# Feed-forward input products of two transformer blocks: high and low activations in one 512-column product, the second half of the bank copied by ScalarE

## The chip, the cores and the metric

The kernel runs as one program on one core of a Trainium2 chip. The metric is the device time of one execution in microseconds (us), the median of several runs. The engines are named as in the profile: PE is TensorE's matmul, PEld its weight load, DVE is VectorE, ACT is ScalarE, POOL is GpSimd, SP is SyncE, which issues most DMAs.

## The reference, cut to what matters

Two blocks of a transformer on one sequence of 256 tokens, D_MODEL = 1024, all in fp32. The first block has four feed-forward parts of this form (D_FF = 2816), before and after its mixers:

```python
def _swiglu(h, w_in, w_out):
    a, b = jnp.split(h @ w_in, 2, axis=-1)
    return (jax.nn.silu(a) * b) @ w_out
```

h is the RMS-normed x (256 x 1024) and w_in is 1024 x 5632. The change touches only the product h @ w_in of these four parts and what directly follows it. The second block's own MLPs (squared ReLU) are not touched.

## The kernel before, in words

**Products in three terms.** Activations and weights are kept as pairs of fp32r tiles, a high part (the value rounded by a copy) and a low part (what the rounding left). A product is the sum of three: high weight x high activation, high weight x low activation, low weight x high activation. For the feed-forward input they are issued by `product` (lines 1878 to 1880) through `two_chunks`, on 256 tokens = 256 columns each. The activations' parts lie in two tiles, `h_hi` and `h_lo`. In the last stage of the program (`mlp_latent`, lines 2448 and 2449) another form is used: activations in one tile `g_both` of two halves, one product of 512 columns for both halves and one of 256 for the low weight, both into one bank.

**Weights in panels.** All weights come as panels of 1 MB (128 x 2048) or 704 KB (128 x 1408, feed-forward outputs), in two buffers. For each panel SP loads `raw`, ACT copies it to `w_hi` in two halves (`hi`, line 617) and DVE subtracts to `w_lo` in two halves (`lo`, line 1057, each after its half of `w_hi`). ACT may write into a buffer only after PE is done with the panel that lay there (`gemm_done`). PE waits for both halves of `w_lo` (`lo_ready`).

**A feed-forward input** has 22 units, one panel each: 128 gate columns a and 128 up columns b, that is 2 x 8 chunks of K x 3 = 48 matmuls. The first unit is peeled (`first_chunks`, lines 1923 to 1925; it goes along with the norm). The others are in a loop of two units per iteration (j = 0 and 1). After each j = 0 unit PE does 64 tiny matmuls of another weight (`ada`, line 1987). a and b of a unit lie in the two halves of one PSUM bank, 0 or 1 by turns. Unit n + 2 may begin when unit n's bank is released (`bank_free`).

**What follows a unit** (`swiglu_evac` on DVE, `swiglu` on ACT) starts when the whole unit is done:

1. DVE: a times the norm's reciprocal (line 1099).
2. ACT: tanh of a/2 (line 704). DVE meanwhile does the low part of the unit before (`low`, line 1086).
3. DVE: (tanh + 1) times a (line 1105), then times b from PSUM (line 1110), which releases the bank.
4. ACT: the copy to the high part of g (line 706).

**The order is written by hand.** The program order of ACT for the unit p is: convert panel p + 1 (two of line 617), tanh of unit p, copy of unit p, then convert panel p + 2. That of DVE is: two of line 1057 for panel p + 1, then the steps of unit p. So the conversion of panel p + 2 on ACT stands behind the copy of unit p on ACT, and on DVE unit p's steps stand behind the low part of panel p + 1.

After 22 units the outputs follow (`out_of`, lines 1966 to 1968), 16 panels of 704 KB with 33 matmuls each.

## Time and profile before

| | |
|---|---|
| median of 3 runs | 2270.43 us (2269.54 to 2276.41) |
| the profiled execution's own time | 2277.8 us |
| its span, first to last instruction | 2276.1 us |
| PE busy, share of the span | 2146.5 us, 94% |
| PEld | 1872.6 us, 82% |
| DVE | 1387.3 us, 61% |
| ACT | 846.5 us, 37% |
| POOL | 38.2 us, 2% |
| granted TensorE clock, mean | 0.965 |
| chain that ended last | PE 82%, DVE 10%, ACT 4% |

The profiled execution took 7.4 us more than the median. Matmuls are pipelined: a row of PE shows the matmul's whole stay, so what counts is the distance of two starts. The same holds, less strongly, on DVE and ACT: an instruction that needs nothing of the one before it starts some 0.08 us before that one's recorded end.

### The profile page before, as it was taken

How to read it: one execution, taken by the hardware profiler on the slowest of the kernel's cores; microseconds unless marked ns; L12 is line 12 of the kernel's file. 1: busy time of each engine (PE TensorE's matmuls, PEld its weight loads, DVE VectorE, ACT ScalarE, POOL GpSimd, SP SyncE). 2: the span in 40 equal slices, each digit the busy share in tenths (PEclk: the TensorE clock that was granted, in tenths of full speed). 3: DMA queues.
4: the chain of work that ended last, by engine and by line, in shares of the span. 5: the costliest groups of instructions: out<-in, count | busy, mean ns of one | idle time of the engine just before them, and what ended most of it. 6: DMA issues, size and time to landing. Idle time of an engine off the chain costs nothing.

```text
span 2276.1 us, 42979 instructions
## 1 busy us (share of the span) xinstructions
PE 2146.5 (94%) x17118; PEld 1872.6 (82%) x17118; DVE 1387.3 (61%) x2295; ACT 846.5 (37%) x1336; POOL 38.2 (2%) x60
## 2 busy tenths in 40 slices
PE   7999899999999998999979999899999989999998
PEld 7999778999999998899966676787887865458987
DVE  6666667666666667766654556674265355557854
ACT  4444534444444443444422434411111223234332
POOL 0000000000000000000010000000000000000000
PEclk9999989999999999999999999999999989799999
DMA  7665325665666632566531110222222222003544
GB/s 267 237 229 200 138 74 185 238 241 183 235 247 209 224 135 94 193 235 234 205 136 38 38 38 20 80 99 86 110 92 93 93 74 92 1 19 114 182 169 144
DMA packets 50227, 325.71 MB, mean 143 GB/s; under 512 B 5328, under 2 KB 8656, under 8 KB 16976
## 3 DMA queue, kind: packets, MB, share of 16 engines
q1 hardware_dynamic: 42480, 266.62, 33.1%
q0 software_dynamic: 7648, 57.71, 6.7%
q8 instruction: 70, 1.15, 0.2%
q14 instruction: 29, 0.24, 0.0%
HBM read 323.26 MB, written 1.05 MB: 142 GB/s over the span
## 4 chain that ended last, share of the span: by engine, by line
PE 82%; DVE 10%; ACT 4%; issue 2%; DMA 0%; DVEq 0%; ACTq 0%; SPq 0%
PE psum L1878 17%; PE psum L1879 16%; PE psum L1880 16%; PE psum L1966 4%; PE psum L1968 3%; PE psum L1967 3%; PE psum L2448 3%; DVE w_lo L1057 3%; PE psum L1987 2%; PE psum L2292 2%; ACT w_hi L617 1%; PE psum L2449 1%; ACT scratch L863 1%; PE psum L2277 1%; PE psum L2312 1%
## 5 line engine op out<-in xcount | busy, mean ns | idle before, releaser
L1057 DVE TENSOR_TENSOR w_lo<-raw,w_hi 128x1024 fp32r<-128x1024 f32 (+1 forms) x542 | 600.0, 1147 | 236.5 <-ACT w_hi L617 221.7
L617 ACT ACTIVATE w_hi<-raw 128x1024 fp32r<-128x1024 f32 (+1 forms) x542 | 514.5, 991 | 574.9 <-PE psum L1880 351.6
L1878 PE MATMUL psum<-h_hi,w_hi 128*128 128x256 f32 (+1 forms) x2136 | 644.4, 302 | 18.2 <-DVE x_res L1217 6.3
L1879 PE MATMUL psum<-h_lo,w_hi 128*128 128x256 f32 (+1 forms) x2136 | 636.4, 298 | 0.0
L1880 PE MATMUL psum<-h_hi,w_lo 128*128 128x256 f32 (+1 forms) x2136 | 635.9, 298 | 0.0
L1878 PEld LDWEIGHTS psum<-h_hi,w_hi 128*128 128x128 f32 x2136 | 413.3, 193 | 39.7 <-issue 17.1
L1880 PEld LDWEIGHTS psum<-h_hi,w_lo 128*128 128x128 f32 x2136 | 413.8, 194 | 10.0
L1879 PEld LDWEIGHTS psum<-h_lo,w_hi 128*128 128x128 f32 x2136 | 413.9, 194 | 9.8
L1966 PE MATMUL psum<-g_both,w_hi 128*128 128x256 f32 x704 | 202.4, 287 | 8.2 <-DVE w_lo L1057 8.2
L1967 PE MATMUL psum<-g_both,w_hi 128*128 128x256 f32 x704 | 199.1, 283 | 0.0
L1968 PE MATMUL psum<-g_both,w_lo 128*128 128x256 f32 x704 | 199.1, 283 | 0.0
L1966 PEld LDWEIGHTS psum<-g_both,w_hi 128*128 128x128 f32 x704 | 134.9, 192 | 13.4 <-DVE w_lo L1057 12.8
L1967 PEld LDWEIGHTS psum<-g_both,w_hi 128*128 128x128 f32 x704 | 134.9, 192 | 0.0
L1968 PEld LDWEIGHTS psum<-g_both,w_lo 128*128 128x128 f32 x704 | 134.9, 192 | 0.0
L704 ACT ACTIVATE scratch<-scratch 128x256 f32<-128x256 f32 x88 | 36.8, 418 | 213.9 <-DVE scratch L1099 213.9
L854 ACT ACTIVATE scratch<-psum 128x512 f32<-128x512 f32 x80 | 43.4, 594 | 171.9 <-PE psum L2292 171.9
L1577 DVE SCALAR_TENSOR_TENSOR x_res<-psum,mods,x_res 128x256 f32<-128x256 f32 (+1 forms) x64 | 28.0, 478 | 129.8 <-PE psum L1880 118.5
L1878 PE MATMUL psum<-g_both,w_hi 128*128 128x512 f32 x256 | 100.3, 392 | 6.1 <-DVE g_both L1718 6.1
L1880 PE MATMUL psum<-g_both,w_lo 128*128 128x512 f32 x256 | 100.3, 392 | 0.0
L1879 PE MATMUL psum<-g_both,w_hi 128*128 128x512 f32 x256 | 100.3, 392 | 0.0
L2448 PE MATMUL psum<-g_both,w_hi 128*128 128x512 f32 x256 | 92.1, 404 | 3.2 <-DVE g_both L1718 3.2
L2449 PE MATMUL psum<-g_both,w_lo 128*128 128x256 f32 x256 | 72.6, 283 | 0.0
(345 smaller groups left out, 3193.4 us busy)
## 6 DMA issues: line engine op xcount, KB each, us to landing
raw<-in_weights SPq DMA_DIRECT2D x207, 1024.0 KB, 4.8
raw_ada<-in_ada POOLq DMA_DIRECT2D x48, 1024.0 KB, 6.7
raw<-in_weights SPq DMA_DIRECT2D x64, 704.0 KB, 4.1
arena<-in_rpb POOLq DMA_DIRECT2D x1, 2048.0 KB, 11.3
arena<-in_fox_c POOLq DMA_DIRECT2D x1, 1696.0 KB, 9.1
const_region<-in_latent_c POOLq DMA_DIRECT2D x1, 1394.0 KB, 7.2
const_region<-in_even_c POOLq DMA_DIRECT2D x1, 1360.0 KB, 8.0
x_res<-in_x_lat SPq DMA_DIRECT2D x4, 256.0 KB, 7.2
```

What stands on the lines that cost most here:

```text
L617: nc.scalar.activation(wh[s][:, a], raw[s][:, a], ACT.Copy).then_inc(hi_ready, 1)
L1057: V.tensor_tensor(wl[s][:, a], raw[s][:, a], wh[s][:, a].bitcast(F32), ALU.subtract).then_inc(lo_ready, 1)
L1878: mm(out, sh, mh, start=n == 0, stop=False)
L1879: mm(out, sh, ml, start=False, stop=False)
L1880: ins = mm(out, sl, mh, start=False, stop=n == len(pairs) - 1)
L1966: mm(out, wh[s][:, a:a + P], gh[:, g0:g0 + T], start=first, stop=False)
L1967: mm(out, wh[s][:, a:a + P], gl[:, g0:g0 + T], start=False, stop=False)
L1968: ins = mm(out, wl[s][:, a:a + P], gh[:, g0:g0 + T], start=False, stop=last)
L1987: ins = mm(psum[r:r + 32, ADA_BANK, 0:64], cond_s[:, c, :], own, start=c == 0, stop=c == DC - 1, tile_position=(0, r))
L2292: ins = nc.tensor.transpose(psum[:, 4 + m, b * P:(b + 1) * P], st_p[:, 2 * (k % 2) + m, b * P:(b + 1) * P], ident)
L2448: mm(out, wh[s][:, a:a + P], g_both[:, :, g0:g0 + T], start=first, stop=False)
L2449: ins = mm(out[:, 0:T], wl[s][:, a:a + P], gh[:, g0:g0 + T], start=False, stop=last)
```

## The change

- The high and low activations lie in one tile `h_both` (two halves), and `h_hi` and `h_lo` are views of it. Other stages use the views as before.
- A unit of the feed-forward inputs now uses two banks, 0 or 1 for the gate and 4 or 5 for the up part. Per chunk of K there is one matmul of 512 columns (high weight with both halves of the activations, into the whole bank) and one of 256 (low weight with the high activations, into the bank's first half). So 32 matmuls instead of 48; the columns are as many as before. All gate matmuls come first, then all up matmuls. The first unit's gate uses bank 3.
- Each result is now the sum of a bank's two halves. ACT copies the second half to SBUF (two new copies per unit), and DVE adds it to the first (two new additions per unit): the gate's sum into `n_add`, the up part's into `e_tmp`. The line that multiplied with b in PSUM now reads `e_tmp`.
- The gate signals on its own (`gate_done`), half a unit before `gemm_done`. The bank is released after the up sum.

```diff
-        hh = sb("h_hi", [P, DC, TJ], F32R)
-        hl = sb("h_lo", [P, DC, TJ], F32R)
+        h_both = sb("h_both", [P, 2, DC, TJ], F32R)
+        hh, hl = h_both[:, 0, :, :], h_both[:, 1, :, :]
...
+        ffn_gl, ffn_ul = n_sq[:, 0, :], n_sq[:, 1, :]
...
             def swiglu(i, j):
 
                 n = pos.n("unit") + 2 * i + j
+                first = isinstance(i, int) and i == 0 and j == 0
+                b = (pos.u + j) % 2
+                act.wait_ge(gate_done, n + 1)
+                nc.scalar.activation(ffn_gl, psum[:, FFN_FIRST if first else b, T:TJ], ACT.Copy).then_inc(gate_low, 1)
                 act.wait_ge(scaled_a, n + 1)
                 nc.scalar.activation(ffn_t[:, j, :], ffn_a[:, j, :], ACT.Tanh, scale=0.5).then_inc(tanh_done, 1)
-                act.wait_ge(bank_free, pos.u + 2 * i + j + 3)
+                act.wait_ge(gemm_done, pos.e + 2 * i + j + 1)
+                nc.scalar.activation(ffn_ul, psum[:, UP + b, T:TJ], ACT.Copy).then_inc(up_low, 1)
+                act.wait_ge(ffn_made, n + 1)
                 nc.scalar.activation(flat(gh, (2 * i + j) * T, T), ffn_g[:, j, :], ACT.Copy).then_inc(g_hi_done, 1)
...
-                    dve.wait_ge(gemm_done, pos.e + 2 * i + j + 1)
-                    V.tensor_tensor(ffn_a[:, j, :], ps_a, n_inv, ALU.mult).then_inc(scaled_a, 1)
+                    dve.wait_ge(gate_low, n + 1)
+                    V.tensor_tensor(n_add, ps_a, ffn_gl, ALU.add).then_inc(gate_sum, 1)
+                    dve.wait_ge(gate_sum, n + 1)
+                    V.tensor_tensor(ffn_a[:, j, :], n_add, n_inv, ALU.mult).then_inc(scaled_a, 1)
...
                     V.scalar_tensor_tensor(ffn_u[:], ffn_t[:, j, :], 1.0, ffn_a[:, j, :], ALU.add,
                                            ALU.mult).then_inc(ffn_seq, 1)
+                    dve.wait_ge(up_low, n + 1)
+                    V.tensor_tensor(e_tmp[:], ps_b, ffn_ul, ALU.add).then_inc(bank_free, 1)
                     dve.wait_ge(ffn_seq, n + 1)
+                    freed(u)
                     if not peeled:
                         dve.wait_ge(g_ready, n - 1)
-                    V.tensor_tensor(ffn_g[:, j, :], ffn_u[:], ps_b, ALU.mult).then_inc(bank_free, 1)
+                    V.tensor_tensor(ffn_g[:, j, :], ffn_u[:], e_tmp[:], ALU.mult).then_inc(ffn_made, 1)
...
+            def wide_chunks(b, s):
+
+                for m, (o, done) in enumerate(((b, gate_done), (UP + b, gemm_done))):
+                    for k in range(DC):
+                        w_hi, w_lo = wtile(s, k, m, 2 * P)
+                        both, low = (psum[:, o, :], w_hi, h_both[:, :, k, 0:T]), (psum[:, o, 0:T], w_lo, hh[:, k, 0:T])
+                        if k < DC - 1:
+                            mm(*both, start=k == 0, stop=False)
+                            mm(*low, start=False, stop=False)
+                        else:
+                            mm(*low, start=False, stop=False)
+                            ins = mm(*both, start=False, stop=True)
+                    ins.then_inc(done, 1)
```

Where the instructions move: DVE in the loop over units, first iteration's j = 0 unit, from the second half of the low weights on. Names: `w_lo` the low weights, `scratch` holds a, tanh, u and g, `norm_blk` holds the reciprocal and the new copies and the gate's sum, `rope_tmp` is `e_tmp`. Before:

```order
L1057 TENSOR_TENSOR w_lo<-raw,w_hi 128x1024 [waits hi_ready]
L1099 TENSOR_TENSOR scratch<-psum,norm_blk 128x256 [waits gemm_done]
...
L1086 TENSOR_TENSOR g_both<-scratch,g_both 128x256
L1078 REGISTER_ALU
L1105 SCALAR_TENSOR_TENSOR scratch<-scratch 128x256 [waits tanh_done,bank_free]
L1110 TENSOR_TENSOR scratch<-scratch,psum 128x256 [waits g_ready,ffn_seq]
```

And with the change:

```order
L1067 TENSOR_TENSOR w_lo<-raw,w_hi 128x1024 [waits hi_ready]
L1109 TENSOR_TENSOR norm_blk<-psum,norm_blk 128x256 [waits gate_low]
L1111 TENSOR_TENSOR scratch<-norm_blk 128x256 [waits gate_sum]
...
L1096 TENSOR_TENSOR g_both<-scratch,g_both 128x256
L1088 REGISTER_ALU
L1117 SCALAR_TENSOR_TENSOR scratch<-scratch 128x256 [waits tanh_done,bank_free]
L1120 TENSOR_TENSOR rope_tmp<-psum,norm_blk 128x256 [waits up_low]
L1088 REGISTER_ALU [waits ffn_seq]
L1125 TENSOR_TENSOR scratch<-scratch,rope_tmp 128x256 [waits g_ready,bank_free]
```

The gate's sum (L1109) still stands behind the low weights of the next panel (L1067), and the scaling (L1111) now waits for a result of its own engine.

ACT at the same unit, before:

```order
L704 ACTIVATE scratch<-scratch 128x256 [waits scaled_a]
L705 REGISTER_ALU
L706 ISA [waits bank_free]
L706 ACTIVATE g_both<-scratch 128x256
L614 ISA
L617 ACTIVATE w_hi<-raw 128x1024 [waits gemm_done,raw_loaded0]
```

And with the change:

```order
L710 ACTIVATE norm_blk<-psum 128x256 [waits gate_done]
L712 ACTIVATE scratch<-scratch 128x256 [waits scaled_a]
L714 ACTIVATE norm_blk<-psum 128x256 [waits gemm_done]
L716 ISA [waits ffn_made]
L716 ACTIVATE g_both<-scratch 128x256
L618 ISA
L621 ACTIVATE w_hi<-raw 128x1024 [waits gemm_done,raw_loaded0]
```

The two copies (L710, L714) stand around the tanh, and the next panel's conversion (L621) still stands last, behind the copy to g's high part (L716).

## Rows read from the trace of the kernel before

**Rows 1.** The page: busy times, chain that ended last.
```profile
PE 2146.5 (94%) x17118; PEld 1872.6 (82%) x17118; DVE 1387.3 (61%) x2295; ACT 846.5 (37%) x1336; POOL 38.2 (2%) x60
PE 82%; DVE 10%; ACT 4%; issue 2%; DMA 0%; DVEq 0%; ACTq 0%; SPq 0%
```

**Rows 2.** Stretches: us, busy time of each engine, clock, DMA share, GB/s. One iteration.
```profile
36.74:49.48 12.74, 12.74 (x167) 12.52 (x161) 8.06 (x14) 5.57 (x8) 0.53 (x1) 1.00 0.62 239
```

**Rows 3.** Timeline of PE, 256-column matmuls of an input unit.
```profile
42.12 0.28 PE L1880 MATMUL psum<-h_hi,w_lo 128*128 128x256 f32 x1
42.24 0.28 PE L1878 MATMUL psum<-h_hi,w_hi 128*128 128x256 f32 x1
42.36 0.28 PE L1879 MATMUL psum<-h_lo,w_hi 128*128 128x256 f32 x1
```

**Rows 4.** Timeline of PE, last stage: first and last of 32 wide matmuls.
```profile
2194.84 0.40 PE L2448 MATMUL psum<-g_both,w_hi 128*128 128x512 f32 x1
2195.07 0.28 PE L2449 MATMUL psum<-g_both,w_lo 128*128 128x256 f32 x1
...
2205.78 0.40 PE L2448 MATMUL psum<-g_both,w_hi 128*128 128x512 f32 x1
```

**Rows 5.** Timeline of ACT, one iteration (start, duration, line, idle before and releaser).
```profile
43.26 0.42 ACT L704 ACTIVATE scratch<-scratch 128x256 f32<-128x256 f32 x1 [3.13 <-DVE scratch L1099]
44.79 0.42 ACT L706 ACTIVATE g_both<-scratch 128x256 f32 x1 [1.11 <-DVE scratch L1110]
45.21 2.01 ACT L617 ACTIVATE w_hi<-raw 128x1024 fp32r<-128x1024 f32 x2
49.03 0.42 ACT L704 ACTIVATE scratch<-scratch 128x256 f32<-128x256 f32 x1 [1.81 <-DVE scratch L1099]
50.56 0.42 ACT L706 ACTIVATE g_both<-scratch 128x256 f32 x1 [1.11 <-DVE scratch L1110]
50.89 1.99 ACT L617 ACTIVATE w_hi<-raw 128x1024 fp32r<-128x1024 f32 x2
```

**Rows 6.** Timeline of DVE, the same iteration.
```profile
42.80 0.42 DVE L1099 TENSOR_TENSOR scratch<-psum,norm_blk 128x256 f32<-128x256 f32 x1 [1.23 <-PE psum L1880]
...
46.30 2.36 DVE L1057 TENSOR_TENSOR w_lo<-raw,w_hi 128x1024 fp32r<-128x1024 f32 x2 [1.57 <-ACT w_hi L617]
48.58 0.42 DVE L1099 TENSOR_TENSOR scratch<-psum,norm_blk 128x256 f32<-128x256 f32 x1
48.92 0.41 DVE L1086 TENSOR_TENSOR g_both<-scratch,g_both 128x256 f32 x1
49.55 0.43 DVE L1105 SCALAR_TENSOR_TENSOR scratch<-scratch 128x256 f32<-128x256 f32 x1 [0.22 <-ACT scratch L704]
50.02 0.42 DVE L1110 TENSOR_TENSOR scratch<-scratch,psum 128x256 f32<-128x256 f32 x1
```

**Rows 7.** One line of ACT: its reads of 128x256 from PSUM (min/median/max ns).
```profile
L737 ACT ACTIVATE arena<-psum,small x9: 467/484/517, 256.2 to 287.1; 128x256 f32<-128x256 f32 x8, 16x256 f32<-16x256 f32 x1
```

**Rows 8.** Waits: who waited for whom: us in total, times, longest.
```profile
DVE scratch L1099 <- PE psum L1880: 51.3, 44, 1.2
```

**Rows 9.** Timeline of ACT, first and last conversions beside the first input's loop.
```profile
26.28 1.99 ACT L617 ACTIVATE w_hi<-raw 128x1024 fp32r<-128x1024 f32 x2
...
159.77 1.46 ACT L617 ACTIVATE w_hi<-raw 128x704 fp32r<-128x704 f32 x2
```

**Rows 10.** Timeline of PE: the first unit and the first output panel that waited.
```profile
29.77 0.39 PE L1878 MATMUL psum<-h_hi,w_hi 128*128 128x256 f32 x1 [1.16 <-DVE w_lo L1057]
...
162.33 0.39 PE L1966 MATMUL psum<-g_both,w_hi 128*128 128x256 f32 x1 [0.94 <-DVE w_lo L1057]
```

More of the change, by code:

```diff
@@ L60 @@
 FIRST = 4
+FFN_FIRST, UP = 3, 4
 def weight_plan():
@@ L240, in build @@
         ada_done = sem("ada_done")
+        gate_done, gate_low, gate_sum = sem("gate_done"), sem("gate_low"), sem("gate_sum")
+        up_low, ffn_made = sem("up_low"), sem("ffn_made")
         ada_turned = sem("ada_turned")
@@ L1093, in evac @@
                     bank = (pos.u + j) % 2
-                    ps_a, ps_b = psum[:, bank, 0:T], psum[:, bank, T:2 * T]
+                    ps_a, ps_b = psum[:, bank, 0:T], psum[:, UP + bank, 0:T]
                     if peeled and j == 0:
                         inverse_norm()
-                        ps_a, ps_b = psum[:, FIRST, 0:T], psum[:, FIRST + 1, 0:T]
-                    dve.wait_ge(gemm_done, pos.e + 2 * i + j + 1)
-                    V.tensor_tensor(ffn_a[:, j, :], ps_a, n_inv, ALU.mult).then_inc(scaled_a, 1)
+                        ps_a = psum[:, FFN_FIRST, 0:T]
+                    dve.wait_ge(gate_low, n + 1)
+                    V.tensor_tensor(n_add, ps_a, ffn_gl, ALU.add).then_inc(gate_sum, 1)
+                    dve.wait_ge(gate_sum, n + 1)
+                    V.tensor_tensor(ffn_a[:, j, :], n_add, n_inv, ALU.mult).then_inc(scaled_a, 1)
                     if not (peeled and j == 0):
@@ L1926, in first_chunks, with first_wide @@
                 return ins
+            def wide_chunks(b, s):
[10 more added lines that the diff above has]
+                    ins.then_inc(done, 1)
+            def first_wide(s):
+                for k in range(DC):
+                    if k == DC - 1:
+                        first_sum()
+                    pe.wait_ge(h_ready, pos.n("h", 1))
+                    for m, (o, done) in enumerate(((FFN_FIRST, gate_done), (UP + pos.u % 2, gemm_done))):
+                        w_hi, w_lo = wtile(s, k, m, 2 * P)
+                        both, low = (psum[:, o, :], w_hi, h_both[:, :, k, 0:T]), (psum[:, o, 0:T], w_lo, hh[:, k, 0:T])
+                        if k < DC - 1:
+                            mm(*both, start=k == 0, stop=False)
+                            mm(*low, start=False, stop=False)
+                        else:
+                            mm(*low, start=False, stop=False)
+                            ins = mm(*both, start=False, stop=True)
+                        if k == DC - 1:
+                            ins.then_inc(done, 1)
             def first_sum():
@@ L1945, in into @@
                     bank(pos.u + 2 * i + j)
-                    chunks = first_chunks if isinstance(i, int) and i == 0 and j == 0 else two_chunks
-                    chunks(psum[:, (pos.u + j) % 2, :], s).then_inc(gemm_done, 1)
+                    if isinstance(i, int) and i == 0 and j == 0:
+                        first_wide(s)
+                    else:
+                        wide_chunks((pos.u + j) % 2, s)
                     if j == 0:
```

## The prediction

> **What bounds the kernel now.** I read the page first: PE is busy 94% of the span and is 82% of the chain that ended last [rows 1]. Then one stretch, an iteration (two units) of a feed-forward input's loop: it takes 12.74 us, PE is busy in all of it at full clock, DVE 8.06 us and ACT 5.57 us [rows 2]. So PE sets the pace there. The matmuls of 256 columns start 0.12 us apart [rows 3]; 96 of them are 11.52 us, and the remaining 1.22 us are the 64 tiny ones of `ada` with the gaps around them. The average unit takes 6.37 us. The four inputs have 4 x 22 = 88 units.
>
> Then the timelines of ACT and DVE, because this engine pair feeds PE, and here one must look at order, not at busy shares. There is a circle through both. From the start of a panel's conversion on ACT (45.21) to the point where DVE is free after the low part (48.58) are 3.37 us [rows 5, 6]. From DVE's first step of a unit to ACT's next conversion are 2.41 us (42.80 to 45.21) and 2.31 us (48.58 to 50.89), mean 2.36 us; one of them has the loop's turn in it. Together 5.73 us per unit if nothing else is waited for. PE's 6.37 us are longer, so DVE waits for PE: 51.3 us in total, 44 times, at most 1.2 us [rows 8]. That is a margin of only 6.37 - 5.73 = 0.64 us per unit. **This small margin decides the case.**
>
> **The change on PE.** It removes three matmuls of 256 columns per chunk of K and puts one of 512 and one of 256 in their place. The same pair exists in the last stage, on a tile of two halves: 31 pairs take 2205.78 - 2194.84 = 10.94 us, 0.353 us each [rows 4], against 3 x 0.12 = 0.36 us [rows 3]. That is 0.007 us less, by 16 pairs and 88 units: 1408 x 0.007 = 9.8 us less work for PE. An iteration would need 32 x 0.353 + 1.22 = 12.52 us, 6.26 us per unit. The columns are as many as before, which is why so little is won by a third fewer matmuls.
>
> The Trainium skill (TensorE: Matmul & The Clock Gate, Back-to-back issue gap) gives a warm matmul of N columns N / 2.4 ns plus 2.5 ns. By it the pair saves one fixed part of 2.5 ns, an estimate of 3.5 us for all 1408. The trace differs: 0.12 us for 256 columns is some 11 ns more than the page gives, and the pair saves about 7 ns.
>
> **The change on DVE and ACT.** Each unit gets two additions on DVE and two copies on ACT. An addition of this shape lasts 0.42 us (as line 1099, which also reads PSUM and SBUF [rows 6]), a copy 0.42 us (as line 706 [rows 5]) up to 0.48 us (as the reads from PSUM in [rows 7]). What matters is what of it lies in the circle:
>
> - Gate copy on ACT: it stands directly behind the conversion, which ends at +2.0 us, while DVE works on the low part until +3.37 us [rows 5, 6]. Hidden, price 0. The early signal of the gate is worth nothing here: the data are there, but DVE's sum stands in its queue behind the low weights of the next panel, and those behind ACT's conversion.
> - Gate sum on DVE: the scaling now waits for it, a result of the same engine. The nearest pair is line 1105 to line 1110, 0.46 us (49.55 to 50.02, 0.47 as printed) [rows 6]. **+0.46 us.**
> - Up copy on ACT: it may start some 0.33 us after the tanh started (as 50.56 to 50.89 [rows 5]) and ends at 0.33 + 0.42 + 0.04 = 0.79 us, signal included. DVE is free for the up sum 0.52 us (tanh to line 1105, 49.03 to 49.55) + 0.34 us (48.58 to 48.92, two independent steps) = 0.86 us after the tanh's start [rows 5, 6]. Hidden; with 0.52 us, the maximum of [rows 7], it costs 0.03 us.
> - Up sum on DVE: it starts 0.34 us behind (tanh + 1) a, and the last product stands 0.46 us behind the up sum, as it stood 0.46 us behind (tanh + 1) a before. **+0.34 us.**
> - The waits: `gate_low`, `up_low`, `ffn_made` replace others. Where an instruction has a second wait, it starts 0.10 us after what it waited for (49.03 + 0.42 to 49.55), with one wait 0.04 us (42.80 + 0.42 to 43.26) [rows 5, 6]. For two new ones that is 0 to 0.12 us; I take 0, since each has one late wait.
>
> The circle becomes 5.73 - 0.01 + 0.46 + 0.34 = 6.52 us (3.36 instead of 3.37 for the conversion, because 48.58 is also the moment when PE was done). It is longer than what PE needs now (6.26) and longer than the unit before (6.37). **So the bound moves from PE to the circle of ACT and DVE**, and PE waits for `w_lo`, 0.5 us per iteration. Behind this wait nothing else of PE is due; the bank's release comes a unit early enough either way.
>
> **The sum.** For the first input the conversion behind unit 0 starts at 26.28 and that of the second output panel at 159.77, 133.49 us later [rows 9]. With the change unit 0's own steps are 0.80 us longer, then come 20 rounds of 6.52 us, and a last one that is 0.93 us shorter, because its panel is of 704 columns (conversion to PE 162.33 - 159.77 = 2.56 us against 29.77 - 26.28 = 3.49 us [rows 9, 10]): 0.80 + 130.4 + 5.59 = 136.8 us, 3.3 us more. PE already waited for exactly this conversion before (0.94 us at 162.33 [rows 10]), so the delay passes to it whole; from then on the outputs are PE's as before. Three more inputs of the same code: 4 x 3.3 = **13.2 us more**. The first unit's reordering costs nothing: it goes along with the norm, and the tanh's table, now loaded behind the gate copy, has the reciprocal to hide under. PE's 9.8 us turn into waiting and are worth nothing. Against the profiled execution's 2277.8 us that is 2291.0; against the median, 2270.43 + 13.2 = 2283.6 us.
>
> Bounds: if both sums pass on 0.04 us earlier (no signal time, 0.42 instead of 0.46), 84 rounds give 6.7 us back: +6.5 us. If both new waits cost 0.06 us more and the up copy 0.03 us, 84 x 0.15 = 12.6 us come on top: +26 us. The forecast's own range is 2277 to 2296.
>
> **The rivals.**
>
> - *PE stays the bound.* The circle is under 6.26 us, 0.26 us shorter than I sum. Then the whole 9.8 us are gained: 2260.6 us. For it: ACT has 5.57 of 12.74 us of work, with the copies 7.3, and DVE 8.06 + 1.7 = 9.8 us, all under 12.52; by busy time alone nothing binds. Against: every step of the circle is read from rows of the same loop, and none is 0.26 us too long. By the page's 2.5 ns this rival's time would be 2266.9 us. Chance 0.11.
> - *The circle binds, but softly.* It is 6.26 to 6.44 us, because some step starts before its predecessor's end more than the rows show: between 9.8 us gained and 6.5 us lost, middle about 2269 us. Chance 0.13.
> - *The new waits are dear.* Register steps and double waits add over 0.15 us per unit, or ACT and PE slow each other in PSUM: over 2296 us, at 0.25 us extra 84 x 0.25 = 21 us on top, 2305 us. For it: the last product now has three waits. Chance 0.08.
> - *The wide product is no faster than two of 256.* Rows 4 speak against it; PE would need 6.37 us per unit, which is still under 6.52, so the forecast stands even then.
>
> **How the numbers follow.** Forecast 0.68, softly 0.13, PE-bound 0.11, dear 0.08. About 0.3% (6.8 us) is what a measurement can tell from no change: 2263.6 to 2277.2. Faster: most of the PE-bound case and the edge of the soft one, 0.10. Same: the rest of the soft case, a weak gain and the forecast's lowest edge, 0.19. Slower: 0.71. The range goes up to the forecast's bound, 2296, and down to 2267, which leaves out the dear case and most of the PE-bound one, somewhat under 0.2.
>
> **What would show it.** In the profile after: an iteration of the inputs takes about 13.04 us instead of 12.74; PE has new idle time before the first matmul of every second unit, released by the low weights on DVE, about 0.5 us each; pairs of matmuls 0.353 us apart; the waits of DVE for the gate's signal gone or nearly; the gate's scaling 0.46 us after its sum, and ACT's conversion 6.5 us after the one before. It is wrong if PE shows no such waits (first rival), or if the step from up sum to the last product is far over 0.46 us (third).

## The result, and the profile after

| | before | with the change |
|---|---|---|
| median, same chip | 2273.42 us (6 runs, 2268.99 to 2279.59) | 2296.06 us (6 runs, 2288.73 to 2298.20) |
| the profiled execution's own time, its span | 2277.8, 2276.1 us | 2296.21, 2294.6 us |
| ratio | | 1.0099, 95% interval [1.0079, 1.0119] |

The kernel is **slower by 22.5 us** (18 to 27 by the interval). The two profiled executions differ by 18.4 us. The forecast was 13.2 us more, with 2296 as the upper end. Sign and mechanism hold, the size does not.

First the page: busy times, the chain that ended last, and the group of the wide matmuls.

```profile
PE 2143.7 (93%) x15710; PEld 1798.0 (78%) x15710; DVE 1450.9 (63%) x2471; ACT 893.9 (39%) x1512; POOL 38.1 (2%) x60
...
PE 60%; DVE 21%; ACT 10%; issue 7%; ACTq 1%; DVEq 0%; DMA 0%; SPq 0%
...
L1950 PE MATMUL psum<-h_both,w_hi 128*128 128x512 f32 x1176 | 431.6, 405 | 20.1 <-DVE w_lo L1067 20.1
```

PE's busy share fell by one point only. The chain tells more: PE was 82% of it [rows 1] and is 60% now, DVE and ACT together went from 14% to 31%. In the inputs more of this chain now runs through the two small engines. The wide matmuls wait 20.1 us for the low weights.

Two iterations of two units in the first input, an early and a later one, and one in the second input (columns as in [rows 2]). They are cut at ACT's conversions:

```profile
37.09:50.10 13.01, 13.01 (x133) 11.20 (x132) 9.51 (x19) 6.75 (x12) 0.53 (x1) 1.00 0.68 243
98.58:111.59 13.01, 12.78 (x131) 10.74 (x130) 9.52 (x19) 6.64 (x12) 0.53 (x1) 1.00 0.67 244
450.52:463.65 13.13, 12.69 (x130) 10.71 (x130) 9.52 (x18) 6.66 (x13) 0.53 (x1) 1.00 0.62 242
```

It was 12.74 us; the forecast was 13.04. The first input has 13.01, the later ones have 13.13. No engine is full in the last two stretches: in the second input PE works 12.69 and DVE 9.52 of 13.13 us. A circle binds, not a busy engine. In the first stretch PE shows no idle time, because it has fallen behind: it began with a wait of 2.25 us (below), and the `ada` matmuls that close its iterations are there 12.50 us apart (38.19 and 50.69), while ACT's rounds already take 13.01. Only from 83.02 on does it wait in every iteration of this input.

The circle itself, in the later stretch of the first input. ACT's timeline:

```profile
99.08 2.01 ACT L621 ACTIVATE w_hi<-raw 128x1024 fp32r<-128x1024 f32 x2
100.99 0.36 ACT L710 ACTIVATE norm_blk<-psum 128x256 f32<-128x256 f32 x1
103.36 0.42 ACT L712 ACTIVATE scratch<-scratch 128x256 f32<-128x256 f32 x1 [2.01 <-DVE scratch L1111]
103.69 0.36 ACT L714 ACTIVATE norm_blk<-psum 128x256 f32<-128x256 f32 x1
105.23 0.42 ACT L716 ACTIVATE g_both<-scratch 128x256 f32 x1 [1.18 <-DVE scratch L1125]
105.55 1.99 ACT L621 ACTIVATE w_hi<-raw 128x1024 fp32r<-128x1024 f32 x2
```

And DVE's, over the same round:

```profile
100.17 2.36 DVE L1067 TENSOR_TENSOR w_lo<-raw,w_hi 128x1024 fp32r<-128x1024 f32 x2 [1.55 <-ACT w_hi L621]
102.45 0.42 DVE L1109 TENSOR_TENSOR norm_blk<-psum,norm_blk 128x256 f32<-128x256 f32 x1
102.90 0.42 DVE L1111 TENSOR_TENSOR scratch<-norm_blk 128x256 f32<-128x256 f32 x1
103.25 0.42 DVE L1096 TENSOR_TENSOR g_both<-scratch,g_both 128x256 f32 x1
103.88 0.42 DVE L1117 SCALAR_TENSOR_TENSOR scratch<-scratch 128x256 f32<-128x256 f32 x1 [0.22 <-ACT scratch L712]
104.23 0.42 DVE L1120 TENSOR_TENSOR rope_tmp<-psum,norm_blk 128x256 f32<-128x256 f32 x1
104.68 0.43 DVE L1125 TENSOR_TENSOR scratch<-scratch,rope_tmp 128x256 f32<-128x256 f32 x1
```

The gate's sum (102.45) starts as soon as the low part lets it, 3.37 us after the conversion. The scaling follows at +0.45, the up sum 0.35 us behind (tanh + 1) a, the last product 0.45 us behind the up sum, and ACT's next conversion 6.47 us after the one before. From here on a **round** is the distance from one conversion's start on ACT to the next one's. Before, two rounds are 7.07 and 5.67 us long (12.74). With the change they are 6.54 and 6.47 us in the first input, 6.57 and 6.56 us in the other three.

What PE does with it, its waits at the first unit behind the peeled one, at a later unit, and at the second output panel.

```profile
30.96 0.80 PE L1950 MATMUL psum<-h_both,w_hi 128*128 128x512 f32 x1 [2.25 <-DVE w_lo L1067]
...
135.07 0.50 PE L1950 MATMUL psum<-h_both,w_hi 128*128 128x512 f32 x1 [0.26 <-DVE w_lo L1067]
...
166.63 0.39 PE L2015 MATMUL psum<-g_both,w_hi 128*128 128x256 f32 x1 [1.29 <-DVE w_lo L1067]
```

The first was 1.16 and the last 0.94 us [rows 10]. In the list of waits, DVE's gate step no longer waits for PE (51.3 us before [rows 8]), and ACT waits less for the scaling (213.9 us before):

```profile
DVE w_lo L1067 <- ACT w_hi L621: 221.8, 164, 7.6
ACT scratch L712 <- DVE scratch L1111: 174.3, 88, 2.2
```

**Where the 22.5 us come from.** The two traces are laid over each other at the conversions. From an input's start to the start of its outputs the changed kernel is 4.0, 5.2, 4.9 and 5.2 us longer in the four inputs, **19.3 us** together. Everything else together is 0.9 us shorter. What stands behind the fourth input, which neither the change nor any experiment touches, differs by up to 12 us between the traces of this document. So for small differences the sums over the four inputs are the finer measure, and they are given below beside the ratios. The remaining 3 us to the median's 22.5 are within its interval and have no place in the trace.

### The profile page after: what moved, and what is told of

The parts are those of the page before. It is cut to its first block, busy times and chain, and to the rows that moved or that the text cites. A ratio compares the mean times of both kernels' runs of the same rounds, so it can differ in the third digit from the quotient of the medians.

```text
span 2294.6 us, 40543 instructions
## 1 busy us (share of the span) xinstructions
PE 2143.7 (93%) x15710; PEld 1798.0 (78%) x15710; DVE 1450.9 (63%) x2471; ACT 893.9 (39%) x1512; POOL 38.1 (2%) x60
## 4 chain that ended last, share of the span: by engine, by line
PE 60%; DVE 21%; ACT 10%; issue 7%; ACTq 1%; DVEq 0%; DMA 0%; SPq 0%
PE psum L1893 10%; PE psum L1895 9%; PE psum L1894 9%; DVE w_lo L1067 7%; ACT w_hi L621 5%; PE psum L2015 4%; PE psum L2016 3%; PE psum L2017 3%; PE psum L2497 3%; DVE scratch L1125 2%; DVE scratch L1111 2%; DVE scratch L1117 2%; ACT scratch L712 2%; PE psum L2341 2%; PE psum L2498 1%
## 5 line engine op out<-in xcount | busy, mean ns | idle before, releaser
L1067 DVE TENSOR_TENSOR w_lo<-raw,w_hi 128x1024 fp32r<-128x1024 f32 (+1 forms) x542 | 600.1, 1148 | 236.5 <-ACT w_hi L621 221.8
L621 ACT ACTIVATE w_hi<-raw 128x1024 fp32r<-128x1024 f32 (+1 forms) x542 | 514.5, 991 | 575.6 <-PE psum L1895 357.3
L1950 PE MATMUL psum<-h_both,w_hi 128*128 128x512 f32 x1176 | 431.6, 405 | 20.1 <-DVE w_lo L1067 20.1
L1951 PE MATMUL psum<-h_both,w_lo 128*128 128x256 f32 x1176 | 331.0, 281 | 0.0
L1950 PEld LDWEIGHTS psum<-h_both,w_hi 128*128 128x128 f32 x1176 | 222.2, 189 | 81.3 <-issue 24.6
L1893 PE MATMUL psum<-h_both,w_hi 128*128 128x256 f32 (+1 forms) x792 | 259.6, 328 | 15.8 <-DVE x_res L1232 6.2
L1894 PE MATMUL psum<-h_both,w_hi 128*128 128x256 f32 (+1 forms) x792 | 256.4, 324 | 0.0
L1895 PE MATMUL psum<-h_both,w_lo 128*128 128x256 f32 (+1 forms) x792 | 256.1, 323 | 0.0
L1951 PEld LDWEIGHTS psum<-h_both,w_lo 128*128 128x128 f32 x1176 | 223.5, 190 | 3.9
L2017 PE MATMUL psum<-g_both,w_lo 128*128 128x256 f32 x704 | 199.0, 283 | 0.0
L1893 PEld LDWEIGHTS psum<-h_both,w_hi 128*128 128x128 f32 x792 | 156.2, 197 | 32.1 <-issue 14.9
L1894 PEld LDWEIGHTS psum<-h_both,w_hi 128*128 128x128 f32 x792 | 156.5, 198 | 10.0
L1895 PEld LDWEIGHTS psum<-h_both,w_lo 128*128 128x128 f32 x792 | 156.2, 197 | 9.9
L1893 PE MATMUL psum<-g_both,w_hi 128*128 128x512 f32 x256 | 101.7, 397 | 6.1 <-DVE g_both L1733 6.1
```

Source lines behind the costliest of these rows:

```text
L621: nc.scalar.activation(wh[s][:, a], raw[s][:, a], ACT.Copy).then_inc(hi_ready, 1)
L1067: V.tensor_tensor(wl[s][:, a], raw[s][:, a], wh[s][:, a].bitcast(F32), ALU.subtract).then_inc(lo_ready, 1)
L1893: mm(out, sh, mh, start=n == 0, stop=False)
L1894: mm(out, sh, ml, start=False, stop=False)
L1895: ins = mm(out, sl, mh, start=False, stop=n == len(pairs) - 1)
L1950: mm(*both, start=k == 0, stop=False)
```

## The experiments

Two theories at the start. **Circle**: the two sums on DVE lengthen the circle of ACT and DVE beyond PE's need, and everything else is hidden. **PE**: the wide product or the new copies cost PE time. Ratios are to the kernel before on the same chip. Sums per input are read from the conversions, as above.

**1. The wide product alone.** On the changed kernel, both copies and both sums out, the signals back to where they were:

```diff
-                act.wait_ge(gate_done, n + 1)
-                nc.scalar.activation(ffn_gl, psum[:, FFN_FIRST if first else b, T:TJ], ACT.Copy).then_inc(gate_low, 1)
...
-                    V.tensor_tensor(n_add, ps_a, ffn_gl, ALU.add).then_inc(gate_sum, 1)
...
-                    V.tensor_tensor(e_tmp[:], ps_b, ffn_ul, ALU.add).then_inc(bank_free, 1)
```

> Edit: the changed kernel's products (512 + 256 columns), but no copies of the banks' second halves on ACT and no sums on DVE: gate and up part are taken from the first halves alone, so the product of high weights with low activations is left out of the result in the feed-forward inputs. Theory (the circle through ACT and DVE binds the changed kernel): without the two sums the circle is 5.73 us per unit, PE's 6.26 us bind, an iteration takes 12.52 us, and the time is 9.8 us below before, ratio 0.996. Rival (the wide product itself costs PE time, by its two-part reading or the switch between widths): not below before, iteration 12.74 us or more. By the Trainium skill's 2.5 ns per matmul (TensorE: Matmul & The Clock Gate, Back-to-back issue gap) the gain would be 3.5 us, an estimate.

2262.42 us, ratio 0.9959 [0.9944, 0.9975], 9.3 us less. One iteration and the chain:

```profile
36.74:49.24 12.50, 12.50 (x129) 10.75 (x129) 7.94 (x14) 5.58 (x8) 0.53 (x1) 1.00 0.64 248
...
PE 82%; DVE 10%; ACT 4%; issue 3%; DMA 0%; DVEq 0%; ACTq 0%; SPq 0%
```

12.50 us against 12.52 forecast. The wide product is worth what the prediction said (9.8 us) where nothing covers it; over the four inputs alone it is 9.0 us. The estimate of 3.5 us is too small here. The PE theory falls for the product.

**2. Narrow products, sums kept.** Three matmuls of 256 columns into the same halves, but for the first unit:

```diff
-                            mm(*both, start=k == 0, stop=False)
-                            mm(*low, start=False, stop=False)
...
+                        mm(psum[:, o, T:TJ], w_hi, hl[:, k, 0:T], start=k == 0, stop=k == DC - 1)
...
+                        mm(psum[:, o, 0:T], w_hi, hh[:, k, 0:T], start=k == 0, stop=False)
+                        ins = mm(psum[:, o, 0:T], w_lo, hh[:, k, 0:T], start=False, stop=k == DC - 1)
```

> Edit: the changed kernel with its copies and sums, but in all units except the first the wide product is split again into two of 256 columns, 48 matmuls per unit. Theory: PE's work rises from 6.26 to 6.37 us per unit, still under the circle's 6.5 us, so the time is the changed kernel's: 19 to 23 us above before, ratio about 1.009, iteration 13.0 to 13.1 us. Rival (the wide product is to blame): the loss goes away, ratio under 1.003.

2296.94 us, ratio 1.0099 [1.0074, 1.0124]: the changed kernel's time. Rounds of 6.535 and 6.468 us, later 6.56. With 48 matmuls or 32, PE waits. Both runs together show that the loss comes with the sums and their copies, and not with the wide product. No run takes out a sum and leaves its copy. That the copies are hidden is read from the timelines: the gate's sum starts 0.08 us before the recorded end of the low part (102.45 against 100.17 + 2.36), as an instruction does that waits for nothing else, and the up sum 0.35 us behind (tanh + 1) a (103.88 to 104.23), the distance of two independent steps.

**3. Without the gate's sum.** The gate's copy and sum out, the scaling reads the bank's first half (the gate is then without its low activations' term):

```diff
-                    dve.wait_ge(gate_low, n + 1)
-                    V.tensor_tensor(n_add, ps_a, ffn_gl, ALU.add).then_inc(gate_sum, 1)
-                    dve.wait_ge(gate_sum, n + 1)
-                    V.tensor_tensor(ffn_a[:, j, :], n_add, n_inv, ALU.mult).then_inc(scaled_a, 1)
+                    dve.wait_ge(gate_done, n + 1)
+                    V.tensor_tensor(ffn_a[:, j, :], ps_a, n_inv, ALU.mult).then_inc(scaled_a, 1)
```

> Edit: the changed kernel without the gate's copy and sum: DVE scales the first half of the gate bank at once (the low activations are left out of the gate in the feed-forward inputs). Theory: 0.46 us leave the circle, 6.5 - 0.46 = 6.06 us, under PE's 6.26: PE binds, iteration 12.52 us, about 8 us below before, ratio 0.996 to 0.998. Rival (PE or PSUM contention, not the circle): a small change, at most the 2 x 0.42 us of load, and still above before.

2260.43 us, ratio 0.993 [0.9913, 0.9946], below the expected 0.996 to 0.998. The four inputs are 6.3 us shorter than before, where the ratio says 15.9 us; the rest has no place in the inputs, and its cause is open. Two rounds are 12.50 us: PE binds. The circle without the 0.45 us is under PE's pace, as the sum says (6.505 - 0.453 = 6.05).

**4. Without the up part's sum.** The last product reads the bank again (the up part without its low activations' term):

```diff
-                    V.tensor_tensor(e_tmp[:], ps_b, ffn_ul, ALU.add).then_inc(bank_free, 1)
+                    dve.wait_ge(gemm_done, pos.e + 2 * i + j + 1)
...
-                    V.tensor_tensor(ffn_g[:, j, :], ffn_u[:], e_tmp[:], ALU.mult).then_inc(ffn_made, 1)
+                    V.tensor_tensor(ffn_g[:, j, :], ffn_u[:], ps_b, ALU.mult).then_inc(bank_free, 1)
```

> Edit: the changed kernel without the up part's copy and sum: the last product reads the first half of the up bank (the low activations are left out of the up part). Theory: 0.34 us leave the circle, and the register step of the later inputs with them: 6.17 us, just under PE's 6.26. Iteration 12.52 us, ratio 0.996 to 0.999. Rival: as for the kernel without the gate's sum.

2263.91 us, ratio 0.9966 [0.9947, 0.9985]. Rounds of 6.285 us in the later inputs, 0.28 us less than 6.565 and not 0.34; two of them are 12.57 us, so the circle still binds there. DVE's timeline there, a j = 0 and a j = 1 unit:

```profile
451.15 0.43 DVE L1115 SCALAR_TENSOR_TENSOR scratch<-scratch 128x256 f32<-128x256 f32 x1 [0.22 <-ACT scratch L712]
451.77 0.42 DVE L1121 TENSOR_TENSOR scratch<-scratch,psum 128x256 f32<-128x256 f32 x1 [0.19 <-DVE scratch L1115]
...
457.43 0.43 DVE L1115 SCALAR_TENSOR_TENSOR scratch<-scratch 128x256 f32<-128x256 f32 x1 [0.22 <-ACT scratch L712]
457.94 0.42 DVE L1121 TENSOR_TENSOR scratch<-scratch,psum 128x256 f32<-128x256 f32 x1
```

The dependent step takes 0.62 and 0.51 us, where the step to the last product takes 0.45 us in the changed kernel's first input. The product has three waits, as in the changed kernel. But the one that is met last, for (tanh + 1) a, does not stand on the product: in the trace's small instructions it stands on a semaphore instruction in front of it, and in the j = 0 unit a register step of 0.08 us stands between the two. **Waits have a price after all.** This was the first sign.

**5. One more addition**, independent, behind the up sum:

```diff
                     V.tensor_tensor(e_tmp[:], ps_b, ffn_ul, ALU.add).then_inc(bank_free, 1)
+                    V.tensor_tensor(scr[:, 2048:2048 + T], ffn_a[:, j, :], n_inv, ALU.add)
```

> Edit: the changed kernel with one more addition of 128x256 on DVE per unit, behind the up sum, into scratch that nobody reads. Theory: it costs at most 0.34 us in the circle; but behind the up sum DVE would only wait 0.46 us for it anyway, of which 0.12 us are then left, so 0.34 to 0.40 us replace 0.12 to 0.20 us of waiting: 0.2 to 0.34 us a unit, 84 rounds, 17 to 28 us above the changed kernel, less than that if the addition lies wholly in the wait. Rival (PE binds): nothing.

2303.74 us, ratio 1.0119 [1.0102, 1.0137]. The rounds grow by 0.21 us in the first input and 0.16 us later, and the four inputs are 15.4 us longer than the changed kernel's. The ratios do not tell the two kernels apart (1.0119 against 1.0099, the intervals overlap), so this rests on the rounds. The expectation was too high. DVE's timeline:

```profile
106.69 0.42 DVE L1120 TENSOR_TENSOR rope_tmp<-psum,norm_blk 128x256 f32<-128x256 f32 x1
107.03 0.42 DVE L1121 TENSOR_TENSOR scratch<-scratch,norm_blk 128x256 f32<-128x256 f32 x1
107.36 0.42 DVE L1126 TENSOR_TENSOR scratch<-scratch,rope_tmp 128x256 f32<-128x256 f32 x1
```

Up sum to last product is 0.67 us with an instruction between and 0.45 us without. An independent instruction is passed on after 0.34 us, a dependent one after 0.45; the one put between hides the difference. So its price in the circle is 0.21 us, less than half of its 0.42 us. The circle theory holds: one more instruction in it, and every round is longer although DVE has some 3 us of idle time per iteration.

**6. A semaphore of its own for the up sum.** In the later inputs the step from up sum to last product is longer than in the first one. Two places of the changed kernel, second input, j = 0 and j = 1:

```profile
449.11 0.42 DVE L1120 TENSOR_TENSOR rope_tmp<-psum,norm_blk 128x256 f32<-128x256 f32 x1
449.65 0.43 DVE L1125 TENSOR_TENSOR scratch<-scratch,rope_tmp 128x256 f32<-128x256 f32 x1
...
455.66 0.42 DVE L1120 TENSOR_TENSOR rope_tmp<-psum,norm_blk 128x256 f32<-128x256 f32 x1
456.11 0.42 DVE L1125 TENSOR_TENSOR scratch<-scratch,rope_tmp 128x256 f32<-128x256 f32 x1
```

0.54 against 0.45 us. I took the bank's count for the cause, whose awaited value is worked out in a register in the loop, and gave the up sum a semaphore with a plain count:

```diff
-                    V.tensor_tensor(e_tmp[:], ps_b, ffn_ul, ALU.add).then_inc(bank_free, 1)
+                    V.tensor_tensor(e_tmp[:], ps_b, ffn_ul, ALU.add).then_inc(up_sum, 1)
                     dve.wait_ge(ffn_seq, n + 1)
-                    freed(u)
+                    dve.wait_ge(up_sum, n + 1)
...
-                    V.tensor_tensor(ffn_g[:, j, :], ffn_u[:], e_tmp[:], ALU.mult).then_inc(ffn_made, 1)
+                    V.tensor_tensor(ffn_g[:, j, :], ffn_u[:], e_tmp[:], ALU.mult).then_inc(bank_free, 1)
```

> Edit: the changed kernel, but the up sum signals on a semaphore of its own that counts like the others of the unit, and the last product releases the bank again. Theory: in the second to fourth input a register step (ALU_OP at the last product, 0.08 us in every second unit) stands between the up sum and the last product, because the bank's count needs a register of its own; without it their rounds go from 6.565 to about 6.52 us: 63 x 0.05 = 3 us below the changed kernel, ratio to before about 1.008. Rival (the 0.06 us per unit by which the later inputs are slower than the first come from elsewhere): rounds unchanged.

A miss: 2299.13 us, ratio 1.0107 [1.0087, 1.0127], rounds 0.05 to 0.07 us longer than the changed kernel's, the four inputs 5.3 us. DVE's timeline of such a j = 0 unit:

```profile
450.52 0.42 DVE L1120 TENSOR_TENSOR rope_tmp<-psum,norm_blk 128x256 f32<-128x256 f32 x1
451.13 0.42 DVE L1125 TENSOR_TENSOR scratch<-scratch,rope_tmp 128x256 f32<-128x256 f32 x1 [0.19 <-DVE rope_tmp L1120]
```

The step is now 0.61 us. The trace's small instructions tell why. The wait for the up sum comes last. In the changed kernel it rides on the product itself in a j = 1 unit (0.45 us) and on the register step, 0.08 us ahead of the product, in a j = 0 unit (0.54 us). Here it stands on a semaphore instruction of its own in front of either: 0.51 and 0.61 us. So a late wait on an instruction of its own costs about 0.06 us more. The Trainium skill says that such instructions are put in front when an instruction waits for several engines (Perfetto Trace Analysis, Identifying Dependency Chains); the trace has them here too, though all three waits are for results of DVE itself, and adds the price.

**7. One wait fewer ahead of the last product.** Its wait for the low part of g, long met, moves one step up:

```diff
+                    if not peeled:
+                        dve.wait_ge(g_ready, n - 1)
                     V.scalar_tensor_tensor(ffn_u[:], ffn_t[:, j, :], 1.0, ffn_a[:, j, :], ALU.add,
...
-                    if not peeled:
-                        dve.wait_ge(g_ready, n - 1)
```

> The changed kernel with one edit: the last product's wait for the low part of g of the unit before moves one step ahead, in front of (tanh + 1) a, where it has long been met. In the changed kernel the last product starts 0.453 us after the up sum in the first input and 0.542 us after it in the j = 0 units of the later ones; there a register step of 0.084 us stands between. Theory (the number of late or register waits ahead of the last product makes this step longer): with one wait fewer there, the rounds of the later inputs fall from 6.565 to 6.505 to 6.52 us, 63 rounds x 0.05 = 3 us less than the changed kernel, a ratio to the kernel before of about 1.008. Rival (the register step comes from the bank's count, whose value is computed in the loop, and stays whatever the other wait does): rounds of 6.56 us, ratio 1.010. A second rival: the wait costs as much at its new place as it did at the old, same rounds.

2291.4 us, ratio 1.006 [1.0039, 1.0082]. DVE's timeline, second input, a j = 0 and a j = 1 unit:

```profile
449.30 0.42 DVE L1122 TENSOR_TENSOR rope_tmp<-psum,norm_blk 128x256 f32<-128x256 f32 x1
449.75 0.42 DVE L1125 TENSOR_TENSOR scratch<-scratch,rope_tmp 128x256 f32<-128x256 f32 x1
...
455.44 0.43 DVE L1119 SCALAR_TENSOR_TENSOR scratch<-scratch 128x256 f32<-128x256 f32 x1 [0.25 <-ACT scratch L712]
```

The long step of 0.54 us is gone (0.45). The moved wait costs 0.03 us in other units, where it now stands behind the tanh's wait (0.25 instead of 0.22 us of idle time). Net: rounds of 6.53 instead of 6.565 us later, but 6.53 instead of 6.505 in the first input. The four inputs are together 0.5 us shorter than the changed kernel's. It was my theory in part, and the second rival in part. The ratio is lower than the changed kernel's by more than this explains, though the intervals overlap; what the rest is, the trace does not show.

**8. The gate's copy waits for the whole unit.** This tests a sentence of the prediction, that the early signal is worth nothing:

```diff
-                act.wait_ge(gate_done, n + 1)
+                act.wait_ge(gemm_done, pos.e + 2 * i + j + 1)
```

> The changed kernel with one edit: ACT's copy of the gate's second half waits for the whole unit's signal instead of the gate's own. Claim of the prediction (the early signal is worth nothing, since the gate's sum stands behind the low weights of the next panel): time as the changed kernel, rounds of 6.505 us in the first input and 6.565 us in the later ones, ratio about 1.010. Rival (the early signal hides the copy: PE's last matmul of a unit ends so close ahead of the low weights' end that a copy that starts only then, and lasts 0.37 us, ends after it in every second unit): 0.1 to 0.2 us per round more, rounds of 6.6 to 6.75 us, 84 x 0.1 to 0.2 = 8 to 17 us over the changed kernel, ratio 1.014 to 1.017.

2304.74 us, ratio 1.0115 [1.0095, 1.0134]. By the conversions the four inputs are 8.9 us longer than with the early signal. ACT's copy and DVE's sum at two places, the second right behind PE's first wait:

```profile
110.78 0.38 ACT L710 ACTIVATE norm_blk<-psum 128x256 f32<-128x256 f32 x1 [1.08 <-PE psum L1954]
...
38.12 0.38 ACT L710 ACTIVATE norm_blk<-psum 128x256 f32<-128x256 f32 x1 [2.41 <-PE psum L1954]
```

```profile
111.19 0.42 DVE L1109 TENSOR_TENSOR norm_blk<-psum,norm_blk 128x256 f32<-128x256 f32 x1
...
38.53 0.42 DVE L1109 TENSOR_TENSOR norm_blk<-psum,norm_blk 128x256 f32<-128x256 f32 x1 [1.38 <-ACT norm_blk L710]
```

The usual unit loses some 0.1 us (111.19 is 2.41 us behind the low part's start, where 2.28 is the rule); one round in each of the first two inputs loses 1.4 to 1.6 us. The rival was right in the rounds (6.62 to 6.70 us on average) and in the 8.9 us, and the prediction's sentence wrong. The ratio is below the rival's 1.014 to 1.017, and its interval overlaps the changed kernel's: this too rests on the rounds of one trace each.

**9. The conversion first, in the kernel before.** The circle can be cut by order alone. ACT's copy to g's high part goes behind the next panel's conversion. At the end of an input DVE's low part of the last unit goes behind the first output panel's low weights with it (not shown):

```diff
+                if not (isinstance(i, int) and i == 0 and j == 0):
+                    g_copy(pos.u + 2 * i + j - 1, 2 * i + j - 1, 1 - j)
                 act.wait_ge(scaled_a, n + 1)
                 nc.scalar.activation(ffn_t[:, j, :], ffn_a[:, j, :], ACT.Tanh, scale=0.5).then_inc(tanh_done, 1)
-                act.wait_ge(bank_free, pos.u + 2 * i + j + 3)
-                nc.scalar.activation(flat(gh, (2 * i + j) * T, T), ffn_g[:, j, :], ACT.Copy).then_inc(g_hi_done, 1)
```

> Edit: the kernel before with one thing moved: on ACT the conversion of panel p + 2 stands ahead of the copy to g's high part of unit p. Theory: the loop is PE's as before (12.74 us per iteration), only the waits at unit 2 and at the second output panel go, 1.4 + 1.1 us by four inputs: about 10 us below before at most, ratio 0.996 to 0.998. This tells how much of the reordered version's gain is the order alone. Rival (those waits only move to the next panel): ratio 1.000.

2260.71 us, ratio 0.9953 [0.9936, 0.9971], 10.7 us less. An iteration stays at 12.74 us; PE's waits at the two ends of an input [rows 10] are gone, 2.1 to 2.2 us in three inputs and 0.9 us in the third. The four inputs are 9.3 us shorter. The ratio is just under the expected 0.996.

**10. The conversion first, with the change.** The same, and the up part's copy, sum and last product move too: behind the tanh of a unit ACT has only the up copy and then the conversion. On DVE the low part of the unit before moves ahead of the gate's sum.

```diff
+            def swiglu_pre(i, j):
+
+                if not (isinstance(i, int) and i == 0 and j == 0):
+                    up_copy(pos.n("unit") + 2 * i + j - 1, 0, pos.e + 2 * i + j, (pos.u + j + 1) % 2)
...
+                if not first:
+                    g_copy(n - 1, 2 * i + j - 1, 1 - j)
                 act.wait_ge(gate_done, n + 1)
...
-                act.wait_ge(ffn_made, n + 1)
-                nc.scalar.activation(flat(gh, (2 * i + j) * T, T), ffn_g[:, j, :], ACT.Copy).then_inc(g_hi_done, 1)
```

> Edit: the changed kernel with another order on ACT and DVE: of unit p only the gate copy, tanh and (tanh + 1) times a stand before the unit's end; the up copy and sum and the last product of unit p stand before the conversion of panel p + 2, and the copy to g's high part behind that conversion. Theory: the circle becomes conversion and low part 3.36 + gate sum 0.46 + scaling to tanh 0.45 + tanh to up copy 0.33 + up copy to conversion 0.33 = 4.9 us, far under PE's 6.26 us. PE binds, iteration 12.52 us: 9.8 us below before, and the waits at the first units and at the second output panel (1.4 and 1.1 us in each of the four) go too, 2.5 x 4 = 10 us at most. In all 14 to 20 us below before, ratio 0.991 to 0.994. Rival (the extra instructions cost by load or by contention in PSUM, not by order): it stays above before.

**2250.97 us, ratio 0.9909 [0.989, 0.9929]: 20.7 us less than the kernel before**, just over the 14 to 20 us expected, and faster than both. One iteration and ACT's timeline:

```profile
100.00:112.50 12.50, 12.50 (x130) 10.73 (x129) 9.84 (x20) 6.77 (x13) 0.53 (x1) 1.00 0.68 252
```

```profile
104.33 0.38 ACT L709 ACTIVATE norm_blk<-psum 128x256 f32<-128x256 f32 x1 [1.06 <-PE psum L1982]
104.61 2.00 ACT L621 ACTIVATE w_hi<-raw 128x1024 fp32r<-128x1024 f32 x2
106.51 0.40 ACT L714 ACTIVATE g_both<-scratch 128x256 f32 x1
```

What ACT does ahead of the conversion, the up copy, now waits for PE's unit alone, and DVE does 9.84 us of work in an iteration of 12.50 without holding anybody up. The sums are all there; only their place in the order changed. The gain is near the sum of experiment 1 (9.3 us) and experiment 9 (10.7 us); over the four inputs alone it is 16.3 us, against 9.0 and 9.3.

## Why the prediction was wrong in its size

- **The bound moves from PE to the circle: right.** Experiments 1 and 2 part the causes, 3 and 4 shorten the circle, 5 lengthens it. The sign that was named for it, some 0.5 us of waiting per iteration, is there too: the step to the unit's first matmul is 0.62 us at 109.05 instead of 0.12, of which the profile shows 0.23 us as idle time.
- **PE's pair of 0.353 us, 9.8 us less work: right** (12.50 us per iteration in experiment 1), and it turned into waiting: 13.01 - 12.50 = 0.51 us per iteration in the first input, once PE has caught up.
- **Gate sum +0.46, up sum +0.34 us: right** (0.453 and 0.342 us). The copies are hidden: right, with 0.36 us even shorter than the 0.42 to 0.52 of the rows they were costed from. By the Trainium skill (VectorE: DVE Perf Modes, The TRN2 errata) a ScalarE copy of 256 elements would take (172 + 256) / 1.2 GHz = 0.357 us out of PSUM and (224 + 256) / 1.2 GHz = 0.40 us out of SBUF, both estimates from its table of cycles; the trace agrees in the first (0.36) and has 0.42 in the second. It was the better price, and changed nothing.
- **The round of 6.52 us: right in the first input** (6.505 us), 0.045 us too short in the others (6.565).
- **"A last one that is 0.93 us shorter, because its panel is of 704 columns": this step failed.** The term belonged to the wrong round. Here are the last two conversions that follow a unit:

```profile
157.61 1.99 ACT L621 ACTIVATE w_hi<-raw 128x1024 fp32r<-128x1024 f32 x2
...
164.07 1.46 ACT L621 ACTIVATE w_hi<-raw 128x704 fp32r<-128x704 f32 x2
```

  The first output panel's conversion, at 157.61, is done in full width (2 x 1024 elements); its round is 6.46 us long. Only the panel behind it is narrow, and that one lies behind the point up to which I counted, before as after. In [rows 9] the narrow one is 159.77, the *second* output panel's; the round that ends there begins with the wide one. So there are 21 full rounds: 0.80 + 21 x 6.52 = 137.7 us against 133.49, +4.2 us per input instead of +3.3, and 4 x 0.93 = **3.7 us** were missing.
- **"For two new ones that is 0 to 0.12 us; I take 0, since each has one late wait": this step failed too.** That a wait is met early does not make it free. In the first input the rounds are 136.60 us together, in the other three 137.62 to 137.84: **3.3 us**. The circle was read from the first input's rows [rows 5, 6] alone and taken for all four. Here is DVE in a j = 0 unit of the second input, before and with the change:

```profile
451.08 0.42 DVE L1099 TENSOR_TENSOR scratch<-psum,norm_blk 128x256 f32<-128x256 f32 x1
...
451.99 0.43 DVE L1105 SCALAR_TENSOR_TENSOR scratch<-scratch 128x256 f32<-128x256 f32 x1 [0.15 <-ACT scratch L704]
452.54 0.42 DVE L1110 TENSOR_TENSOR scratch<-scratch,psum 128x256 f32<-128x256 f32 x1
```

```profile
447.79 0.43 DVE L1111 TENSOR_TENSOR scratch<-norm_blk 128x256 f32<-128x256 f32 x1
...
448.77 0.43 DVE L1117 SCALAR_TENSOR_TENSOR scratch<-scratch 128x256 f32<-128x256 f32 x1 [0.22 <-ACT scratch L712]
```

  Against the changed kernel's first input two things are longer: a register step stands between up sum and last product, 0.09 us in every j = 0 unit, and ACT's loop turn is 0.02 us longer. But this register step is not the change's. The kernel before has it at the same place, with two waits on the product: 0.55 us from 451.99 to 452.54, against 0.46 us in the first input. What the change adds there is at the tanh. Before, the wait for it rides on (tanh + 1) a in the later inputs, which starts 0.91 us after the scaling. With the change it stands on a semaphore instruction of its own, as in the first input of both kernels: 0.98 us (0.97 to 0.98 in those). So the price of the waits is 0.07 us per unit in the later inputs and next to nothing in the first. The mean of the given bounds, 0.06 us per unit, would have been right there. 0.2 of the 3.3 us are one round of the second input in which PE was late (last section).
- Together: 13.2 + 3.7 + 3.3 = 20.2 us; unit 0 takes 0.87 instead of 0.80 us (+0.3), the rounds of the first input's kind 6.505 instead of 6.52 us (84 x 0.015 = -1.3): 19.2 us, against 19.3 us measured from conversion to conversion. What the median shows beyond that, some 3 us, is left open.
- **"The early signal of the gate is worth nothing here": wrong.** It is worth 8.9 us by the conversions (experiment 8), some 3 us of them in two rounds in which PE's clock was low. The sentence looked at the queue only: the sum stands behind the low weights, and these are done later than the unit. But with the late signal the copy starts after the unit's end, and copy and signal (0.41 us) reach beyond the low part. I had costed the copy as "directly behind the conversion", which the early signal makes true. It did not harm the sum, since the change has the early signal.
- Range and chances: 2296.06 lies just above the range's upper end, 2296, which was built from 0.15 us of unknown costs per round. The two missed terms, 7 us, took more than half of that reserve. 3 us more lie in the base: the forecast counts from 2270.43 us, and the kernel before took 2273.42 us in the comparison. As a difference, 22.5 us is within the bounds of 6.5 to 26 us that were given.

## What to carry to other kernels

Where two small engines hand work to each other in a fixed program order, add up the circle, not the busy shares: an instruction in it costs its start-to-start step, although DVE is idle for a quarter and ACT for half of the time. Before adding work to such a circle, ask which step of it really has to stand ahead of the next panel's conversion; here moving the others behind it turned a loss of 22.5 us into a gain of 20.7 us, of which the same move alone, without the change, brings 10.7 us. And count rounds from the rows: which panel each round converts, in which width, up to the very mark that the rows give.

## What the runs showed of the hardware

- **A dependent step on DVE costs 0.45 us, an independent one 0.34 us** (0.42 us instructions, 128x256). The Trainium skill (VectorE: DVE Perf Modes, The DRAIN you can't avoid) says of a chain of copies that a semaphore after each costs nothing extra. The runs here differ where an instruction waits for the one just before it: 0.11 us. An independent instruction between takes this back (experiment 5).
- **Which wait rides on the instruction matters.** The same dependent step took 0.45 us with the late wait on the instruction itself, 0.51 us with it on a semaphore instruction in front (experiments 4 and 6), 0.54 us with it on a register step in front (changed kernel, j = 0), and 0.61 us with semaphore instruction and register step both in front (experiment 6).
- **After a long wait PE's clock was halved, and it cost next to nothing.** In the first input PE waits 2.25 us until 30.96, and then:

```profile
31.00:34.40 3.40, 3.40 (x11) 2.92 (x12) 2.35 (x7) 1.38 (x4) 0.00 (x0) 0.53 0.61 205
34.40:37.00 2.60, 2.60 (x17) 2.25 (x16) 1.90 (x2) 1.89 (x3) 0.00 (x0) 1.00 0.33 139
```

  The granted clock is 0.53, near the 1.2 GHz level, for 3.4 us, then 2.4 GHz again. The kernel before has 1.00 in the same stretch. ACT's rounds do not show it (6.56 and 6.47 us), because PE is not in the circle. The second input has the same fall after a wait of 2.32 us (388.39). PE is then so late that at 402.70 the up copy waits 0.22 us for it, and one round takes 6.78 instead of 6.57 us. In the fourth input a wait of 2.32 us (956.42) was followed by no fall at all. In experiment 8, where the gate's copy waits for PE's last matmul, PE is in it, and the same drop makes that round 7.93 us long.
